# mLSTM prompt/sample kernel: the sample states' matmuls stand between the K steps of the next projections, and attention's last stores are asked for ahead of the late weight loads

## The chip, the core and the metric

One core of one Trainium2 chip runs the whole kernel in one launch. The metric is device time in microseconds (us) from one execution of it. TensorE (PE) does matmuls, VectorE (DVE) and ScalarE (ACT) evict and scale, GpSimd (POOL) does elementwise work and issues a few transfers, SyncE (SP) issues nearly all others.

## What is computed

A decoder layer for a prompt of 2048 tokens (with 16 meta tokens ahead) and, with the same weights, 8 sample sequences of 8 tokens each:

```
p = RMSNorm_pre(x) @ w_in + b_in        # q_a k_a v_a z_a | q_m k_m v_m o_m z_m i_m f_m | g_a g_b
y_a = sliding_window_attention(...) * silu(z_a)               # 16 heads, 4 kv heads
# mLSTM, 4 heads of width 256, per chunk; C0 is the matrix memory (256 x 256), n0 its normaliser
num = a * (q @ C0) + (W * q k^T) @ v
den = a * (q @ n0) + rowsum(W * q k^T)
h   = num / max(|den|, exp(-m))
C1  = aL * C0 + (k * wL)^T @ v ;  n1 = aL * n0 + sum(k * wL)
y_m = sigmoid(o_m) * h * silu(z_m)
out = x + RMSNorm_post((sigmoid(g_a) * (y_a @ w_pa) + sigmoid(g_b) * (y_m @ w_pb)) @ w_out)
```

Every sample sequence has its own C0 and n0 for each mLSTM head (32 states of 256 x 256), which are read, used, updated and stored. The prompt starts at zero and carries one state per head through its 17 tiles.

## The kernel before

The rows are 17 tiles of 128. Tile 0 is the mixed one: 16 meta tokens in rows 0 to 15, the 64 sample rows in rows 64 to 127 (`S0 = 64`); tiles 1 to 16 are the prompt. There are four stages, one after the other: `prelude` (norm, gates), `mlstm` (4 heads x 17 tiles), `attention` (4 kv heads x 17 tiles) and `tail` (merge and output products). Every engine has its own program, in order, and only semaphores tie them together; nothing is scheduled for them.

In `mlstm` each engine walks through slots (h, t), with n = 17 h + t. In slot n, PE first projects tile n+1 in three blocks (`block_a`: q and k into bank `p_a`; `block_b`: v and o into `p_b`; `block_c`: z into `p_c`), and between the blocks it does tile n: transposes of q and k (L1118), the product q k^T (L1126), then the reads of the state and the sum over the tile into `p_n` (L1142, L1143) and the update of the state into `p_u` (L1147). A block is 8 K steps; a K step is three matmuls (L642 to L644: high by high, high by low, low by high part), 512 columns wide in blocks a and b and 256 in block c. A [128 x 128] by 257-column fp32 matmul is two records in the profile.

Slot t = 0 is different (`mixed_tile`). After block_c come the tile's own sum (L1152), the meta tokens' update of the prompt state (L1157), and then, for each of the 8 sequences b, two matmuls that read its state into `p_n` (L1166: the weights `qz` hold q of that sequence alone in 64 columns, the output is rows 64 to 127) and two that make its update (L1179: 64 rows of `kwz` by `vaug`) into `p_u`, or into `p_a` and `p_b` for even b. DVE applies each update to `cs` (L1017) and moves the normaliser column in and out (`ncol`, L1058; L1025). Only then does PE go on to slot 1, whose `block_a` comes first. I call the two reads or the two updates of one sequence a pair: 16 pairs a head, 64 in all.

DVE in slot t = 0: `evict_a`, `qat` (L976), `wlog` (L978), eight copies into `qz` (L985), `evict_b`, ..., the copies of the meta update into `cn` (L1008, semaphore `c_ready`), the 8 sequences' updates, then the denominator and `y` (L1028 to L1038).

POOL in slot n makes the low part of tile n+2's h (`pool_split_h`, L635; slot n+1's `block_a` waits for it). In slot t = 0 of heads 0 to 2 it waits until the 8 states are stored (`cs_out`) and issues the loads of the next head's 8 (`load_states`, L889). Then it prepares weights for `tail`, two or three chunks a slot (`prepare`, L910 to L925). SP stores a sample state when its update is ready, in slot t = 0 (L802), loads h, stores y, and so on, in one queue.

At the end of `attention`, SP's slot t = 16 of the last head asks for the rest of the tail's first weights (8 transfers, 6 MB, `k.late_in`), then stores the last keys and values, then the last `y`; it waits for the landing of those stores (L1383, L1384) before the barrier ahead of `tail` (L2639). PE waits for `late_in` at its fifth product.

Of the kernel before, what the change touches and what calls it, by code (L numbers as in the profile page):

```python
# [54 lines left out]
W_COLS = 5 * MD  # L55
STG = 4
# [582 lines left out]
def project(nc, out, hi, lo, k, col, n):  # L639

    for j in range(KT):
        nc.tensor.matmul(out, hi[:, j], k.w_hi[:, j, col:col + n], start=(j == 0), stop=False)  # L642
        nc.tensor.matmul(out, hi[:, j], k.w_lo[:, j, col:col + n], start=False, stop=False)  # L643
        last = nc.tensor.matmul(out, lo[:, j], k.w_hi[:, j, col:col + n], start=False, stop=(j == KT - 1))  # L644
    return last


def mlstm(nc, k):
# [3 lines left out]
    with ExitStack() as ctx:  # L652
# [28 lines left out]
        qz = sb("ml_qz", [P, NB, JD, NB * DT])  # L681
# [20 lines left out]
        qz_ready, kwz_ready, us_done, cs_ready = sem("qz_ready"), sem("kwz_ready"), sem("us_done"), sem("cs_ready")  # L702
        qz_clear = sem("qz_clear")
# [8 lines left out]
        last_n = MH * NT - 1  # L712
        block = ctx.enter_context(nc.Block())
# [16 lines left out]

        def sample_banks(b):

            return p_u if b % 2 else [p_a, p_b]
# [8 lines left out]
        def _(sp):  # L742
# [24 lines left out]
            def slot(h, t, n, u, half):  # L767
# [30 lines left out]
                if isinstance(t, int) and t == 0:  # L798
# [85 lines left out]
        def _(pool):  # L884
            nc.gpsimd.memset(qz[:, :, :, :], 0.0).then_inc(qz_clear, 1)
# [46 lines left out]
        def _(dve):  # L932
# [28 lines left out]
            def slot(h, t, n, u, half):  # L961
# [40 lines left out]
                if tile0:  # L1002
# [7 lines left out]
                    for b in range(NB):  # L1010
                        c = NB * h + b
                        if b == 0:
                            for bb in range(2):
                                ncol(NB * h + bb)
                        dve.wait_ge(us_done, c + 1)
                        for j in range(JD):
                            q = V.scalar_tensor_tensor(out=cs[:, b, j, :], in0=cs[:, b, j, :],  # L1017
                                                       scalar=k.al_smp[:, b, h:h + 1],
                                                       in1=sample_banks(b)[j][:, 0:MD + 1],
                                                       op0=ALU.mult, op1=ALU.add)  # L1020
                        q.then_inc(cs_ready, 1)
                        if b + 2 < NB:
                            ncol(c + 2)
                        dve.wait_ge(cs_ready, c + 1)
                        V.tensor_copy(nout[:, :, b * MH + h], cs[:, b, :, MD]).then_inc(nout_ready, 1)  # L1025
# [14 lines left out]
                if not tile0:  # L1040
# [12 lines left out]
            def ncol(c):  # L1053

                b, h = c % NB, c // NB
                if h:
                    dve.wait_ge(nout_ready, (NB + 1) * (h - 1) + b + 1)
                V.tensor_copy(cs[:, b, :, MD], k.n0_col[:, :, b * MH + h]).then_inc(ncol_ready, 1)  # L1058
# [11 lines left out]
        def _(pe):  # L1070
# [6 lines left out]
            def proj_ab(h, n, u, bank, col, width, done, free, nchunks):  # L1077
# [6 lines left out]
                project(nc, bank[:, 0:width], k.h_hi[:, u], k.h_lo[:, u], k, col, width).then_inc(done, 1)  # L1084

            def block_a(h, n, u, new):
                proj_ab(h, n, u, p_a, A, 2 * MD, proj_a, qk_ready, 4 if new else None)

            def block_b(h, n, u, new):
# [16 lines left out]
            def slot(h, t, n, u, half):  # L1106
# [4 lines left out]
                if more:  # L1111
                    block_a(hn, n + 1, 1 - u, last)
# [1630 lines left out]
```

## Time and profile before

| | |
|---|---|
| median of 3 runs | 3233.28 us (3232.41, 3233.28, 3253.26) |
| the profiled execution | 3260.61 us, span 3258.7 us |
| PE busy | 3099.0 us, 95% of the span |
| DVE, POOL, ACT busy | 1485.8, 1264.9, 1040.1 us |
| mean granted TensorE clock | 0.953 of full |

The profile is of one execution, which took 27.3 us longer than the median of the runs. The span is from the first to the last instruction; the other 1.9 us lie around it. A busy share is no measure of need: at half clock PE is busy twice as long for the same work.

### The profile page before, as it was taken

To read this page: it belongs to the slowest core of one execution; us is meant where nothing else is said; L and a number is where in the kernel's file an instruction comes from. 1 tells how busy PE (TensorE), PEld (TensorE's weight loads), DVE (VectorE), ACT (ScalarE), POOL (GpSimd) and SP (SyncE) were. 2 spreads that over 40 slices of the span, in tenths; PEclk is the share of its full clock that TensorE was granted. 3 is DMA by queue.
4 is the path that set the end of the run, shared out by engine and by line. 5 is a ranking of instruction groups with operands and counts; after the bars stand their busy time and mean duration, and the time that the engine had idled before them with its cause. 6 is when DMAs were issued, how large, how long until landed. Compare 5 with 4: busy or idle time off the path is not lost. (4 is left out here: it accounts for less than half of the span.)

```text
span 3258.7 us, 51503 instructions
## 1 busy us (share of the span) xinstructions
PE 3099.0 (95%) x17011; PEld 2648.1 (81%) x17011; DVE 1485.8 (46%) x3684; ACT 1040.1 (32%) x2450; POOL 1264.9 (39%) x938
## 2 busy tenths in 40 slices
PE   5799999999899999989999999999979999999898
PEld 4578877888688878878989989989868787878787
DVE  3323342335333523345455555545445464546487
ACT  5211121113111311124444444434423333333343
POOL 2235544554445535211212212212244444546566
PEclk8789997999999979999999999989989999999999
DMA  8644454435634534241121121141152847377843
GB/s 251 186 141 145 145 166 159 141 133 149 206 127 144 161 120 146 77 124 54 54 74 62 56 79 56 48 145 56 54 212 108 331 161 293 122 273 248 298 155 136
DMA packets 259046, 472.27 MB, mean 145 GB/s; under 512 B 29778, under 2 KB 138855, under 8 KB 255812
## 3 DMA queue, kind: packets, MB, share of 16 engines
q1 hardware_dynamic: 254692, 461.08, 42.0%
q0 software_dynamic: 2880, 8.93, 0.9%
q8 instruction: 70, 1.15, 0.1%
q10 hardware_dynamic: 1344, 0.62, 0.1%
q14 instruction: 60, 0.49, 0.1%
HBM read 316.15 MB, written 156.38 MB: 145 GB/s over the span
## 5 line engine op out<-in xcount | busy, mean ns | idle before, releaser
L635 POOL TENSOR_TENSOR a_all<-h_raw,a_all 128x1024 fp32r<-128x1024 f32 x137 | 329.1, 2402 | 803.9 <-issue 453.9
L839 ACT ACTIVATE ml_qkt<-ml_pt 128x512 f32<-128x512 f32 x68 | 40.8, 600 | 974.3 <-PE ml_pt L1118 974.3
L2418 DVE TENSOR_TENSOR a_all<-tl_sums,a_all 128x512 fp32r<-128x512 f32 x165 | 186.4, 1130 | 219.7 <-ACT a_all L2314 218.5
L642 PE MATMUL ml_pa<-w_all,a_all 128*128 128x512 f32 x544 | 230.8, 424 | 25.9 <-issue 17.1
L943 DVE TENSOR_TENSOR ml_qk<-ml_pa,ml_bias 128x512 f32<-128x512 f32 x68 | 47.1, 692 | 425.7 <-ACT ml_kw L843 420.7
L642 PE MATMUL ml_pb<-w_all,a_all 128*128 128x512 f32 x544 | 217.5, 400 | 3.4 <-issue 3.4
L644 PE MATMUL ml_pa<-w_all,a_all 128*128 128x512 f32 x544 | 217.5, 400 | 0.0
L643 PE MATMUL ml_pa<-w_all,a_all 128*128 128x512 f32 x544 | 217.4, 400 | 0.0
L644 PE MATMUL ml_pb<-w_all,a_all 128*128 128x512 f32 x544 | 212.1, 390 | 0.0
L643 PE MATMUL ml_pb<-w_all,a_all 128*128 128x512 f32 x544 | 212.0, 390 | 0.0
L1401 POOL TENSOR_TENSOR at_vs<-at_qkv,ones 128x64 f32<-128x64 f32 x68 | 22.0, 323 | 475.9 <-PE at_bank_po L1765 466.0
L1443 ACT ACTIVATE at_sm<-at_sm,at_nmx 128x272 f32<-128x272 f32 x272 | 138.8, 511 | 180.3 <-DVE at_nmx L1592 180.3
L925 POOL TENSOR_TENSOR w_early<-prep_raw,w_early 128x512 fp32r<-128x512 f32 x140 | 188.5, 1346 | 11.2
L642 PE MATMUL at_bank_pa<-w_all,a_all 128*128 128x384 f32 x544 | 189.2, 348 | 0.0
L627 ACT ACTIVATE a_all<-h_raw 128x1024 fp32r<-128x1024 f32 x137 | 144.0, 1052 | 127.8 <-DMA h_raw<-h_t 127.8
L643 PE MATMUL at_bank_pa<-w_all,a_all 128*128 128x384 f32 x544 | 181.9, 334 | 0.0
L644 PE MATMUL at_bank_pa<-w_all,a_all 128*128 128x384 f32 x544 | 181.9, 334 | 0.0
L2574 PE MATMUL tl_bank_y<-w_all,a_all 128*128 128x512 f32 x416 | 167.0, 401 | 13.0 <-DMA w_all<-w_split 13.0
L642 PE MATMUL at_bank_pb<-w_all,a_all 128*128 128x256 f32 x544 | 165.0, 303 | 3.0 <-PEq L652 3.0
L2577 PE MATMUL tl_bank_y<-w_all,a_all 128*128 128x512 f32 x416 | 164.8, 396 | 0.0
L2576 PE MATMUL tl_bank_y<-w_all,a_all 128*128 128x512 f32 x416 | 164.8, 396 | 0.0
L642 PE MATMUL ml_pc<-w_all,a_all 128*128 128x256 f32 x544 | 159.1, 292 | 0.0
(406 smaller groups left out, 8657.9 us busy)
## 6 DMA issues: line engine op xcount, KB each, us to landing
h_raw<-h_t SPq DMA_DIRECT2D x140, 512.0 KB, 4.3
w_split<-w_early SPq DMA_DIRECT2D x140, 512.0 KB, 3.0
w_all<-w_split SPq DMA_DIRECT2D x36, 1024.0 KB, 11.2
stage<-w_in_in SPq DMA_DIRECT2D x35, 512.0 KB, 7.2
w_early<-w_split SPq DMA_DIRECT2D x14, 1024.0 KB, 10.1
stage_more<-w_in_in SPq DMA_DIRECT2D x21, 512.0 KB, 7.3
w_all<-w_split SPq DMA_DIRECT2D x20, 512.0 KB, 10.5
tl_w<-w_split SPq DMA_DIRECT2D x10, 1024.0 KB, 8.3
```

The lines of the kernel that those rows point to most:

```text
L627: nc.scalar.activation(k.h_hi[:, u], k.h_raw[:, u], ACT.Copy).then_inc(k.h_hi_ready, 1)
L635: nc.gpsimd.tensor_tensor(k.h_lo[:, u], k.h_raw[:, u], k.h_hi[:, u].bitcast(F32), ALU.subtract).then_inc(k.h_lo_ready, 1)
L642: nc.tensor.matmul(out, hi[:, j], k.w_hi[:, j, col:col + n], start=(j == 0), stop=False)
L643: nc.tensor.matmul(out, hi[:, j], k.w_lo[:, j, col:col + n], start=False, stop=False)
L644: last = nc.tensor.matmul(out, lo[:, j], k.w_hi[:, j, col:col + n], start=False, stop=(j == KT - 1))
L925: G.tensor_tensor(prep_split[:, c % 2, 1], prep_raw[:, j], prep_split[:, c % 2, 0].bitcast(F32), ALU.subtract).then_inc(prep_lo, 1)
L943: V.tensor_tensor(qk[:, :], p_a[:, :], bias[:, h % 2, A:B], ALU.add).then_inc(qk_ready, 1)
L1443: nc.scalar.activation(sm[:, g, :], sm[:, g, :], ACT.Exp, bias=nmx[:, g:g + 1], scale=HD ** -0.5, accum_out=rs[:, g:g + 1]).then_inc(exp_r ...
L2418: V.tensor_tensor(a_part(q, 1), operand(g, j), hi, ALU.subtract).then_inc(a_lo, 1)
L2574: T.matmul(bank_of(bank, at), hi, w_row(at, 0, t), start=fresh and t == 0, stop=False, skip_group_check=True)
L2576: T.matmul(bank_of(bank, at), hi, w_row(at, 1, t), start=False, stop=False, skip_group_check=True)
L2577: last = T.matmul(bank_of(bank, at), lo, w_row(at, 0, t), start=False, stop=t == KH - 1, skip_group_check=True)
```

## The change

In mLSTM the two matmuls that read the state of sequence b move in slot 0 from behind block_c to a place between K steps: b = 0 to 4 ahead of K steps 3 to 7 of `block_b`, b = 5 to 7 ahead of K steps 0 to 2 of `block_c`. The first one now starts the accumulation in `p_n` over all 128 rows (its weights have zeros in the other columns), and the tile's own sum ends it. The two matmuls of the update of sequence b move to slot 1, ahead of K step b of its `block_a`, and all go into `p_u`, each half with a semaphore of its own. PE's program of mLSTM is written out instead of looped.

With that: DVE fills `qz` in one copy and the normaliser column in one (ahead of `evict_b`), applies the updates after `y`, and copies the new normalisers out in one; SP stores the sample states in slot 1; POOL loads the next head's states in slot 4. In attention SP asks for the last `y` store first and for the eight late loads after it, and the waits for the landing of the stores move into `tail`.

```diff
-            nc.gpsimd.memset(qz[:, :, :, :], 0.0).then_inc(qz_clear, 1)
+            nc.gpsimd.memset(qz[:, :], 0.0).then_inc(qz_clear, 1)
...
                 pool_split_h(nc, k, n + 2, u, (proj_c, n + 1))
-                if isinstance(t, int) and t == 0 and h + 1 < MH:
+                if isinstance(t, int) and t == 4 and h + 1 < MH:
+                    pool.wait_ge(nout_ready, 2 * h + 1)
                     pool.wait_ge(cs_out, 16 * NB * (h + 1))
                     load_states(h + 1)
...
-                    for b in range(NB):
-                        q = V.tensor_copy(qz[:, b, :, DT * b:DT * (b + 1)], qat[:, :, S0 + DT * b:S0 + DT * (b + 1)])
-                    q.then_inc(qz_ready, 1)
+                    V.tensor_copy(own_rows, qat[:, :, S0:P].rearrange("p j (b t) -> p b j t", t=DT)).then_inc(qz_ready, 1)
+                    if h:
+                        dve.wait_ge(nout_ready, 2 * (h - 1) + 1)
+                    V.tensor_copy(cs[:, :, :, MD], n0_head(h)).then_inc(ncol_ready, 1)
...
-                if not tile0:
+                if tile0:
+                    for b in range(NB):
+                        c = NB * h + b
+                        for j in range(JD):
+                            dve.wait_ge(us_done if j else us_half, c + 1)
+                            V.scalar_tensor_tensor(out=cs[:, b, j, :], in0=cs[:, b, j, :],
+                                                   scalar=k.al_smp[:, b, h:h + 1], in1=p_u[j][:, 0:MD + 1],
+                                                   op0=ALU.mult, op1=ALU.add).then_inc(cs_ready if j else cs_half, 1)
...
-                    block_a(hn, n + 1, 1 - u, last)
+                    block_a(hn, n + 1, 1 - u, last, (lambda j: state_updates(h, j)) if t == 1 else None)
+                if t == 1:
+                    pe.sem_inc(u_done, 1)
...
-                    block_b(hn, n + 1, 1 - u, last)
+                    block_b(hn, n + 1, 1 - u, last, (lambda j: sample_rows(h, n, j - 3)) if tile0 else None)
...
+            def sample_rows(h, n, b):
+                if not 0 <= b < NB:
+                    return
+                if b == 0:
+                    pe.wait_ge(qz_ready, h + 1)
+                    pe.wait_ge(ncol_ready, h + 1)
+                    pe.wait_ge(cs_in, 16 * NB * (h + 1))
...
+            def state_updates(h, b):
+                c, n = NB * h + b, NT * h
+                pe.wait_ge(n_done, n + 1)
+                pe.wait_ge(kwz_ready, c + 1)
+                for j in range(JD):
                     if b == 0:
                         pe.wait_ge(c_ready, n + 1)
                     else:
-                        pe.wait_ge(cs_ready, c - 1)
...
+                        pe.wait_ge(cs_ready if j else cs_half, c)
+                    T.matmul(p_u[j][:, 0:MD + 1], kwz[S0:P, b, j * P:(j + 1) * P], k.vaug[S0:P, n % 2, :],
+                             start=True, stop=True).then_inc(us_done if j else us_half, 1)
-            run_steps(pe, MH, slot)
+            all_steps(MH, slot)
...
             sp.dma_start(y_dram(KVH - 1, NPT), yt[:, last_m % 2]).then_inc(y_out[last_m % 2], 16)
-            for s in y_out:
-                sp.wait_ge(s, 16 * (last_m + 1) // 2)
-            sp.wait_ge(kv_out, 16 * KVH * (2 * NB + 4))
+            sp.wait_ge(proj_a, last_m + 1)
+            sp.wait_ge(proj_b, last_m + 1)
+            for slot in range(4, N_PAIR):
+                for part in range(2):
+                    load_block(sp, k, 0, slot, part, None, k.late_in)
```

PE, end of slot 0 and start of slot 1 of head 0, before (`ml_pn` is the bank p_n, `ml_pu`, `ml_pa` and `ml_pb` are p_u, p_a and p_b):

```order
192 L644 MATMUL ml_pc<-w_all,a_all 128x256
193 L1152 MATMUL ml_pn<-vaug,ml_wqk 128x257
194 L1157 MATMUL ml_pu<-vaug,ml_kw 128x257 x2
195 L1166 MATMUL ml_pn<-ml_cs,ml_qz 64x257 x2
196 L1179 MATMUL ml_pa<-vaug,ml_kwz 128x257
197 L1179 MATMUL ml_pb<-vaug,ml_kwz 128x257
198 L1166 MATMUL ml_pn<-ml_cs,ml_qz 64x257 x2
199 L1179 MATMUL ml_pu<-vaug,ml_kwz 128x257 x2
```

The same place in the changed kernel:

```order
201 L647 MATMUL ml_pc<-w_all,a_all 128x256
202 L1173 MATMUL ml_pn<-vaug,ml_wqk 128x257
203 L1179 MATMUL ml_pu<-vaug,ml_kw 128x257 x2
204 L1193 MATMUL ml_pu<-vaug,ml_kwz 128x257 x2
205 L645 MATMUL ml_pa<-w_all,a_all 128x512
206 L646 MATMUL ml_pa<-w_all,a_all 128x512
207 L647 MATMUL ml_pa<-w_all,a_all 128x512
208 L1193 MATMUL ml_pu<-vaug,ml_kwz 128x257 x2
```

No read stands there any more, and each pair of updates is followed by a K step of the next tile's block_a. The first pair still stands right behind the meta update.

PE in block_b of slot 0, in the changed kernel (before, these are K steps alone):

```order
150 L645 MATMUL ml_pb<-w_all,a_all 128x512
151 L646 MATMUL ml_pb<-w_all,a_all 128x512
152 L647 MATMUL ml_pb<-w_all,a_all 128x512
153 L1168 MATMUL ml_pn<-ml_cs,ml_qz 128x257
154 L1168 MATMUL ml_pn<-ml_cs,ml_qz 64x257
155 L645 MATMUL ml_pb<-w_all,a_all 128x512
156 L646 MATMUL ml_pb<-w_all,a_all 128x512
157 L647 MATMUL ml_pb<-w_all,a_all 128x512
158 L1168 MATMUL ml_pn<-ml_cs,ml_qz 64x257 x2
```

The first read, 128 rows of output wide, stands ahead of K step 3 and waits for DVE's copies and the loaded states; all that follows in block_b is queued behind it.

POOL in head 0, slot 0 before, where the loads of head 1's states stand ahead of the next tile's low part (`a_all`):

```order
25 L635 TENSOR_TENSOR a_all<-h_raw,a_all 128x1024
26 L889 DMA ml_cs<-state_C_in 128x2x256 x8
27 L635 TENSOR_TENSOR a_all<-h_raw,a_all 128x1024
28 L923 CAST w_early<-prep_raw 128x512
29 L925 TENSOR_TENSOR w_early<-prep_raw,w_early 128x512
```

POOL in the changed kernel, slots 4 and 5 of head 0:

```order
46 L636 TENSOR_TENSOR a_all<-h_raw,a_all 128x1024
47 L897 DMA ml_cs<-state_C_in 128x2x256 x8
48 L932 CAST w_early<-prep_raw 128x512
49 L934 TENSOR_TENSOR w_early<-prep_raw,w_early 128x512
50 L919 TENSOR_TENSOR prep_raw<-prep_raw 128x512
51 L932 CAST w_early<-prep_raw 128x512
52 L934 TENSOR_TENSOR w_early<-prep_raw,w_early 128x512
53 L636 TENSOR_TENSOR a_all<-h_raw,a_all 128x1024
```

The loads and a slot's weight preparation now stand together between two low parts.

## Rows read from the trace of the kernel before

**Rows 1.** Who waited for whom, PE: total us, times, longest
```profile
PE ml_pa L642 <- issue: 17.1, 3, 10.6
```
**Rows 2.** Windows, one a head: slot 0's L1152 to slot 2's L1099
```profile
147.07:211.55 64.48, 59.77 (x189) 38.60 (x187) 17.42 (x54) 4.20 (x8) 15.47 (x15) 0.68 0.37 119
479.42:544.07 64.65, 59.94 (x189) 38.35 (x188) 17.20 (x54) 4.20 (x8) 22.32 (x22) 0.68 0.55 175
811.96:868.05 56.09, 42.96 (x188) 30.53 (x187) 17.64 (x54) 4.20 (x8) 22.34 (x22) 0.91 0.74 232
1135.94:1195.03 59.09, 56.62 (x188) 36.55 (x187) 16.88 (x54) 4.04 (x8) 17.88 (x15) 0.71 0.40 137
```
**Rows 3.** Timeline, PE, ordinary tiles of head 0: start us, us, what
```profile
408.63 1.03 PE L1142 MATMUL ml_pn<-ml_cn,ml_qat 128*128 128x257 f32 x4
409.50 0.59 PE L1143 MATMUL ml_pn<-vaug,ml_wqk 128*128 128x257 f32 x2
...
416.27 0.38 PE L1099 MATMUL ml_pc<-ident,ml_y 128*128 128x128 f32 x2
...
433.33 0.38 PE L1099 MATMUL ml_pc<-ident,ml_y 128*128 128x128 f32 x2
```
**Rows 4.** Timeline, PE, sample loop of head 2, at full clock
```profile
814.70 1.05 PE L1166 MATMUL ml_pn<-ml_cs,ml_qz 128*64 128x257 f32 x4 [1.08 <-DVE ml_cs L1058]
...
828.04 1.05 PE L1166 MATMUL ml_pn<-ml_cs,ml_qz 128*64 128x257 f32 x4 [0.86 <-DVE ml_cs L1058]
...
832.82 0.49 PE L642 MATMUL ml_pa<-w_all,a_all 128*128 128x512 f32 x1 [0.59 <-PE ml_pu L1179]
```
**Rows 5.** Timeline, PE, sample loop of head 0 and block_a behind it
```profile
160.28 1.97 PE L1166 MATMUL ml_pn<-ml_cs,ml_qz 128*64 128x257 f32 x4
...
181.64 0.63 PE L642 MATMUL ml_pa<-w_all,a_all 128*128 128x512 f32 x1
182.92 0.63 PE L642 MATMUL ml_pa<-w_all,a_all 128*128 128x512 f32 x1
```
**Rows 6.** Timeline, slot 0 of head 2: K step 3, DVE's qz copies
```profile
805.25 0.39 PE L642 MATMUL ml_pb<-w_all,a_all 128*128 128x512 f32 x1
...
805.72 0.71 DVE L985 COPY ml_qz<-ml_qat 128x16 f32<-128x16 f32 x8
```
**Rows 7.** Tile ml_cs to 150 us; head 0: last load, K step 3
```profile
DMA to landing us min/median/max: 5.3/6.7/8.1
...
136.42 1.44 POOL L889 DMA_DIRECT2D ml_cs<-state_C_in  x2 [7.70 <-issue]
...
140.36 0.39 PE L642 MATMUL ml_pb<-w_all,a_all 128*128 128x512 f32 x1
```
**Rows 8.** Timeline: state loads (last of head 0's; head 2); ordinary slot
```profile
200.03 0.74 POOL L889 DMA_DIRECT2D ml_cs<-state_C_in  x1 [5.46 <-issue]
...
840.62 2.16 POOL L889 DMA_DIRECT2D ml_cs<-state_C_in  x3 [12.75 <-DMA o_s_c<-ml_cs]
...
851.49 1.44 POOL L889 DMA_DIRECT2D ml_cs<-state_C_in  x2 [3.29 <-issue]
...
623.71 0.58 PE L642 MATMUL ml_pa<-w_all,a_all 128*128 128x512 f32 x1
...
634.16 2.38 POOL L635 TENSOR_TENSOR a_all<-h_raw,a_all 128x1024 fp32r<-128x1024 f32 x1 [9.16 <-issue]
```
**Rows 9.** Windows, POOL alone: a low part and three chunks
```profile
634.10:645.60 11.50, 10.85 (x9) 1.00 0.46 146
```
**Rows 10.** Timeline and one line of code, end of attention
```profile
2359.71 2.42 SPq L1954 DMA_DIRECT2D w_all<-w_split  x4
2362.17 9.44 SPq L1951 DMA_DIRECT2D w_all<-w_split  x4
...
2365.51 0.38 ACT L1493 ACTIVATE at_yt<-at_bank_pb 128x256 f32<-128x256 f32 x1 [5.00 <-PE at_bank_pb L1707]
...
L1383 SPq EVENT_SEMAPHORE  x1: 4999/4999/4999, 2375.1 to 2375.1; - x1
```

More of the change, by code:

```diff
@@ L55 @@
 W_COLS = 5 * MD
+QZ_DIAG = JD * NB * DT + 2 * DT
 STG = 4
@@ L636, in pool_split_h, with project @@
                             ALU.subtract).then_inc(k.h_lo_ready, 1)
-def project(nc, out, hi, lo, k, col, n):
+def project(nc, out, hi, lo, k, col, n, between=None):
     for j in range(KT):
+        if between is not None:
+            between(j)
         nc.tensor.matmul(out, hi[:, j], k.w_hi[:, j, col:col + n], start=(j == 0), stop=False)
@@ L797, in slot @@
                         load_chunk(sp, k, k.ML[h] + 10 + c)
-                if isinstance(t, int) and t == 0:
+                if isinstance(t, int) and t == 1:
                     for b in range(NB):
@@ L1009, in slot @@
                     q.then_inc(c_ready, 1)
[L1010 to L1025, printed above, removed]
                 dve.wait_ge(n_done, n + 1)
@@ L1075, in weights, with proj_ab @@
                 pe.wait_ge(k.w_lo_ready, k.ML[h] + done)
-            def proj_ab(h, n, u, bank, col, width, done, free, nchunks):
+            def proj_ab(h, n, u, bank, col, width, done, free, nchunks, between=None):
                 if nchunks is not None:
@@ L1083, in proj_ab, with block_a, block_b, block_c @@
                     pe.wait_ge(free, n)
[L1084 to L1089, printed above, removed]
-                proj_ab(h, n, u, p_b, B, 2 * MD, proj_b, vo_ready, 8 if new else None)
-            def block_c(h, n, u, new):
-                proj_ab(h, n, u, p_c, C, MD, proj_c, z_ready, 10 if new else None)
+                project(nc, bank[:, 0:width], k.h_hi[:, u], k.h_lo[:, u], k, col, width,
+                        between).then_inc(done, 1)
+            def block_a(h, n, u, new, between=None):
+                proj_ab(h, n, u, p_a, A, 2 * MD, proj_a, qk_ready, 4 if new else None, between)
+            def block_b(h, n, u, new, between=None):
+                proj_ab(h, n, u, p_b, B, 2 * MD, proj_b, vo_ready, 8 if new else None, between)
+            def block_c(h, n, u, new, between=None):
+                proj_ab(h, n, u, p_c, C, MD, proj_c, z_ready, 10 if new else None, between)
             def y_transposed(n):
@@ L1130, in slot @@
                         pe.wait_ge(yt_ready, n)
-                    block_c(hn, n + 1, 1 - u, last)
+                    block_c(hn, n + 1, 1 - u, last, (lambda j: sample_rows(h, n, 5 + j) if j < 3 else None) if tile0 else None)
                 pe.wait_ge(wqk_ready, n + 1)
@@ L1356, in slot @@
                             load_block(sp, k, 0, slot, part, None, early_in)
-                if is_last(t) and a + 1 == KVH:
-                    sp.wait_ge(proj_a, m + 1)
-                    sp.wait_ge(proj_b, m + 1)
-                    for slot in range(4, N_PAIR):
-                        for part in range(2):
-                            load_block(sp, k, 0, slot, part, None, k.late_in)
                 if isinstance(t, int) and t == 0:
@@ L2086, in load_raw @@
                 s, t, n = g // N_ITEM, tile_rows(g)[0], len(tile_rows(g))
+                if g == N_ITEM * PA:
+                    for y_out in k.at_y_out:
+                        sp.wait_ge(y_out, 16 * KVH * NT // 2)
                 if s == OUT:
@@ L2210, in _ @@
             sp.wait_ge(single_out, 16 * 3)
+            sp.wait_ge(k.at_kv_out, 16 * KVH * (2 * NB + 4))
         @block.gpsimd
```

60 lines of the change are left out of this document (26 added, 34 removed).

## Prediction, made before the changed kernel was run

> **What bounds the kernel now.** I read the shares of the engines on the page first: PE is busy for 3099.0 of 3258.7 us, DVE for 46%, POOL for 39%, ACT for 32%. So PE bounds it, and there is no other engine whose saved time would shorten anything by itself. A busy PE is still not a fast PE, so the next view was the granted clock by slice, which is below full in slices of mLSTM; then PE's own waits, where one line stands out among projections, 17.1 us in 3 waits [rows 1]; then one window for each head from L1152 in slot 0 to L1099 in slot 2, which takes in everything that the change moves in mLSTM. The four windows last 64.48, 64.65, 56.09 and 59.09 us at a granted clock of 0.68, 0.68, 0.91 and 0.71 [rows 2]: three heads run the sample work near half clock (1.2 GHz of 2.4), head 2 near full.
>
> What would that stretch last without sample work? An ordinary tile repeats every 17.06 us (L1099 at 416.27 and 433.33), and from the tile's own read to the L1099 behind it is 7.64 us, of which the read pair takes 0.87 [rows 3]. So 7.64 − 0.87 + 17.06 = 23.8 us. The four windows sum to 244.3; 4 × 23.8 = 95.3 would be needed. **149.0 us** lie above it. They are the 64 read pairs and 64 update pairs, DVE waits ahead of them, half clock in them and in the block_a behind them, and the three gaps of [rows 1], which stand ahead of slot 2's block_a: there POOL's low part comes late, since POOL issues eight state loads ahead of it. The sum takes all 149.0 away and puts back what the changed kernel needs.
>
> **Part 1, the pairs: +76.8.** At full clock a pair of 257-column matmuls with 128 rows and columns takes 0.87 [rows 3]. In head 2's sample loop 16 pairs run from 814.70 to 832.82 = 18.12 us, less waits of 0.86 and 0.59 = 16.67, or 1.04 a pair [rows 4]. Each pair there is followed by one of another tile shape (64 output columns, then 64 contraction rows), so I read 0.17 as the price of one change of shape. In the changed kernel every pair stands between K steps of full shape: two changes, 0.87 + 2 × 0.165 = 1.20, and 64 pairs (8 reads and 8 updates in each of 4 heads) make 76.8. The lower end is one change's price for both, about 0.95 to 1.04: 61 to 67. The upper end is that the next weights can't be loaded under such a matmul: half as much again as the loop's 1.04, 1.6 a pair, 102. I take 1.20, since it is nearest to the row with the same operands. One 128-row read a head changes nothing.
>
> The Trainium skill ("TensorEngine Tiling (Array Packing)", Key Properties) says that changing the tiling mode needs TensorE drained first, without a price. By it the 0.17 is the drain and the alternation costs it 128 times, as above; if the drain of a 512-column matmul is longer than that of a 257-column one, the sum would be the upper end. No row before the change shows it between these projections.
>
> **Part 2, new waits inside the projections: +7.2 and +2.2.** The first read of a head stands ahead of K step 3 of block_b and waits for DVE. In head 2 that K step starts at 805.25, and DVE begins the qz copies at 805.72 [rows 6]; now one copy does (a few tenths: I take 0.2) and one for the normaliser column (0.16), so it is ready near 806.1. That is 0.85 of PE idle a head, 3.4 in all; all later K steps queue behind it. DVE's evict_b starts some tenths later, which block_a of the next slot hides. The first update of a head waits for DVE's copies of the meta update (`c_ready`). Head 2 waited 1.08 behind that update, for those copies and a normaliser column [rows 4]; without the column, 0.13, that is 0.95 a head, 3.8. Later updates wait for DVE's update of the half before, which has a K step (0.68 at full clock) and the other half to be done in, so nothing. Before them DVE has y to make, about 1.1 us behind `c_ready`, against 0.87 + 0.68 on PE: covered, by 0.4. 3.4 + 3.8 = 7.2.
>
> Head 0 has one more: its states. POOL issues the last two loads at 136.42 for 1.44 us and a load lands 5.3 to 8.1 us after its issue [rows 7], so at 142.4 to 144.2 at the earliest; PE gets to K step 3 of block_b at 140.36 [rows 7], where before it needed these states only at 160.28 [rows 5]. That is a stall of 2.1 to 3.8; about 2.0 beyond the 0.85, and 0.2 for a qz memset one fifth longer, which stands ahead of the loads: **+2.2**.
>
> **Part 3, POOL's loads in slot 4: +5.5.** The three gaps go, as slot 0 and 1 now have a low part and preparation only. But in slot 4 POOL issues the loads: 840.62 to 851.49 + 1.44 = 12.3 us in head 2 [rows 8], and up to 17.4 in head 0, where the last of them alone had 5.46 of issue ahead of it [rows 8]. It then prepares two or three chunks; a low part and three chunks fill 11.50 us [rows 9], 2.4 of it the low part [rows 8], so 9.1 for three and 6 for two. In an ordinary slot the low part starts 634.16 − 623.71 = 10.5 us behind the slot's first matmul and takes 2.38 [rows 8]: it ends at 12.8. The next low part is needed two slots on, at 2 × 17.06 = 34.1. Head 1 has three chunks in slot 4: 12.8 + 12.3 + 9.1 + 2.4 = 36.6, 2.5 late. Head 0 and 2 have two: 12.8 + 15 to 17 + 6 + 2.4 = 36 to 38 in head 0, 2 to 4 late; 33.5 in head 2, in time. With a half-clock tail behind one of them I put **+5.5**; the ends are 0 (POOL idles enough in the slots before to be early) and 17.1, the old gaps again. The wait for `cs_out` is met: SP stores the states in slot 1 and they land in slot 2. SP's 32 stores there cost it 0.4 each, and its load of h is not due until slot 3.
>
> **Part 4, end of attention: −1.8.** Now SP issues the late loads from 2359.71 for 2.42 + 9.44 = 11.9 us, then the last y store, and waits 5.0 us for its landing, from 2375.1 to 2380.1 [rows 10], and the tail begins behind that. In the changed kernel yt is ready at 2365.9 [rows 10], the store goes first, then 11.9 + 0.6 of issue: SP is free at 2378.4 instead of 2380.1. The late loads start 6 us later and land near 2387; PE wants them at its fifth product, near 2393. Bounds: −6, if what bounds the barrier is ready when the store would be, and +3, if loads of bias and raw rows come late behind them.
>
> **Part 5, PE's loops written out: 0.** Tail's PE is written out already and its slots are full; ordinary tiles in the loop repeat at the same 17.06 as those outside it.
>
> **The sum.** 3260.6 − 149.0 + 76.8 + 7.2 + 2.2 + 5.5 − 1.8 = **3201.5**, with every head at full clock. Will they be? At half clock a pair lasts 1.97 [rows 5] and a K step 1.28 (181.64 to 182.92 [rows 5]), against 0.68. Three heads of four had fallen by the time of their loop, one, with a wait of the same size [rows 4], had not. That wait stays, at the same place; what stood behind it was a stretch of pairs alone, and now stands K steps' 512 columns. I take one head to fall there: 8 × (1.97 − 1.20) + 8 × (1.28 − 0.68) = 6.2 + 4.8 = 11, and 2 until it rises, **+13**. Forecast: **3214.5**.
>
> The profiled execution lies 27.3 us above the median. If heads 0 and 1 had run as head 2 did, each window would be 8.5 shorter, and head 3 about 15 shorter (it has no gap behind it): that makes 3228 for an all-full-clock execution, and the three runs of 3232 to 3253 lie between it and 3260.6. So I take the 27 us to be clock in stretches whose old price the sum has removed whole, and don't shift the forecast by it.
>
> **Rivals.** (1) Full clock throughout, and the 27 us lie elsewhere in the kernel: 3201.5 less up to 27: 3175 to 3200. Head 2 speaks for it: sample work alone doesn't lower the clock. Against it: heads 0, 1 and 3. (2) Changes of shape are dear: 1.6 a pair, 102 − 77 = +25: 3240. The loop's 0.17 speaks against it, but it is a change between two small shapes. (3) The other side, slower: the wait for qz in block_b (0.85 us, more in head 0) lowers the clock there, and it stays low through reads, block_c, meta update, its wait and the updates up to the y transposes. Then each of four heads pays 8 × 0.77 + 8 × 0.6 = 11 for reads and their K steps and 13 for the updates, near 24: 4 × 24 = 97, 3201.5 + 97 = 3298. It is slower than 3266 if more than 64 us are lost so, that is if three heads run both parts at half clock. Against it: an idle PE of 0.86 in head 2's loop left the clock high [rows 4]. (4) The change doesn't do what it says for the gaps: all 17.1 come back in slot 6: 3201.5 + 11.6 + 13 = 3226.
>
> **Chances.** Forecast (3201 to 3228) 0.55; rival 1 0.22; rival 2 0.10; rival 3 0.08; rival 4 0.05. A measurement of this kernel can tell about 1%, 32 us: faster is below 3201, slower above 3266. Faster: rival 1, and a quarter of the forecast's case, where no head falls: 0.36. Slower: rival 3, 0.08. Same: 0.56. The range 3188 to 3243 holds the forecast's case, rival 2 and 4, and half of rival 1.
>
> **What would show it.** In the profile after: reads in block_b 1.88 apart (1.20 + 0.68) at full clock and 3.3 at half; PE idle of 0.8 ahead of the first read, 2 to 4 in head 0; the gaps ahead of slot 2's block_a gone, and small ones ahead of slot 6's; four windows of L1152 to slot 2's L1099 near 23.8 + 9.6 + 1 = 34 us each (40 for one that falls); PE's idle time between attention and tail 1.8 us shorter. The prediction is wrong if a pair between K steps costs over 1.4 at full clock, if two or more heads fall (13 each), if the weight loads of a K step behind a small matmul are exposed, or if POOL is more than 5 us late in slot 6.

## The result and the profile after

The changed kernel takes 3254.55 us (median of 20 runs, 3233.08 to 3267.51), the kernel before 3236.31 (20 runs, 3213.89 to 3264.79): a ratio of 1.005 with a 95% interval of 1.0026 to 1.0074. It is slower by a little, where 3214.5, a gain of 22 us, was forecast. The profiled execution took 3259.87 us with a span of 3258.0; the profile before was of 3260.61.

Most terms of the sum can be read in the profile after. First the PE timeline of head 0 and head 1 around the reads and the first updates:

```profile
144.14 1.25 PE L1168 MATMUL ml_pn<-ml_cs,ml_qz 128*128 128x257 f32 x4 [2.41 <-DMA ml_cs<-state_C_in]
145.32 0.77 PE L645 MATMUL ml_pb<-w_all,a_all 128*128 128x512 f32 x1
...
146.87 1.97 PE L1168 MATMUL ml_pn<-ml_cs,ml_qz 128*64 128x257 f32 x4
148.78 0.50 PE L645 MATMUL ml_pb<-w_all,a_all 128*128 128x512 f32 x1
...
474.90 1.25 PE L1168 MATMUL ml_pn<-ml_cs,ml_qz 128*128 128x257 f32 x4 [0.72 <-DVE ml_qz L993]
...
476.99 1.08 PE L1168 MATMUL ml_pn<-ml_cs,ml_qz 128*64 128x257 f32 x4
...
478.91 1.08 PE L1168 MATMUL ml_pn<-ml_cs,ml_qz 128*64 128x257 f32 x4
...
494.99 1.10 PE L1193 MATMUL ml_pu<-vaug,ml_kwz 64*128 64x257 f32 x4 [1.87 <-POOL a_all L636]
496.02 0.50 PE L645 MATMUL ml_pa<-w_all,a_all 128*128 128x512 f32 x1
...
496.92 2.08 PE L1193 MATMUL ml_pu<-vaug,ml_kwz 64*128 64x257 f32 x4
498.92 0.79 PE L645 MATMUL ml_pa<-w_all,a_all 128*128 128x512 f32 x1
...
500.50 2.08 PE L1193 MATMUL ml_pu<-vaug,ml_kwz 64*128 64x257 f32 x4
```

A read pair and its K step repeat every 478.91 − 476.99 = 1.92 us, so a pair costs 1.92 − 0.68 = 1.24 at full clock: the 1.20 of the sum, against 1.04 in the old loop [rows 4]. In head 0 the 2.41 us wait for the states is followed by a few us at half clock (K step and pair at 145.3 to 148.8), and then the clock rises again although narrow reads (64 output columns) still stand there. The updates go another way. One pair after the wait of 1.87 the period is 500.50 − 496.92 = 3.58 us and stays so to the end of block_a. The windows view of that stretch (duration, PE busy, instructions, granted clock, DMA share, GB/s):

```profile
496.92:521.89 24.97, 24.97 (x51) 0.50 0.11 43
```

PE is busy without a pause and has half its clock. That happens in all four heads of this execution. The waits view, PE:

```profile
PE tl_bank_x L2583 <- PEq L2649: 14.4, 1, 14.4
...
PE ml_pu L1193 <- POOL a_all L636: 6.0, 2, 4.1
...
PE ml_pn L1168 <- DMA ml_cs<-state_C_in: 2.4, 1, 2.4
...
PE ml_pn L1168 <- DVE ml_qz L993: 2.2, 3, 0.7
...
PE ml_pu L1193 <- DVE ml_cn L1018: 2.0, 2, 1.0
```

The first line is the wait between attention and tail. The three gaps ahead of slot 2 are gone ([rows 1] has them). In their place is a wait ahead of the first update pair: 0.94 and 1.01 in heads 0 and 3, for `c_ready` as before, but 1.87 and 4.08 in heads 1 and 2 for POOL's low part of tile 2, which the prediction didn't foresee. Its cause stands on the SP and ACT timelines of head 1, slot 0:

```profile
467.55 3.42 SPq L746 DMA_DIRECT2D ml_bias<-b_in_in  x5
471.07 5.47 SPq L210 DMA_DIRECT2D stage_more<-w_in_in  x4
476.63 7.92 SPq L210 DMA_DIRECT2D stage<-w_in_in  x4
484.64 1.69 SPq L620 DMA_DIRECT2D h_raw<-h_t  x1
...
491.36 1.06 ACT L628 ACTIVATE a_all<-h_raw 128x1024 fp32r<-128x1024 f32 x1 [13.72 <-DMA h_raw<-h_t]
```

SP asks for 13 pieces of the next head's biases and weights first, for 16.8 us, and only then for h. It lands at 491.3, ACT and POOL need 1.06 and 2.34 us more, and block_a waits. In head 2 POOL is held longer still: it waits 23.2 us for the landing of a store of prepared weights, which SP asks for behind the same 13 requests and h. Before, the same queue stood there, and the sample loop, 17 to 31 us long, hid it.

The windows view once more, from block_b of slot 0 (head 0) or slot 0's y transposes (heads 1 to 3) to slot 2's y transposes, which takes in reads, updates and all waits of both kernels. After:

```profile
139.42:211.44 72.02, 68.67 (x241) 45.03 (x240) 20.58 (x49) 9.30 (x21) 9.90 (x7) 0.76 0.38 116
471.31:540.09 68.78, 66.19 (x245) 44.03 (x244) 19.27 (x49) 9.57 (x22) 19.41 (x18) 0.80 0.59 174
800.29:873.72 73.43, 68.64 (x246) 45.45 (x245) 19.91 (x49) 9.57 (x22) 16.81 (x14) 0.77 0.61 184
1132.19:1201.60 69.41, 67.68 (x246) 44.81 (x245) 21.10 (x49) 9.57 (x22) 18.17 (x15) 0.78 0.51 158
```

Before, the same stretches:

```profile
138.20:211.55 73.35, 68.64 (x242) 46.51 (x240) 20.95 (x70) 9.32 (x21) 15.47 (x15) 0.72 0.47 141
469.99:544.07 74.08, 69.37 (x246) 46.83 (x245) 20.73 (x70) 9.58 (x22) 24.45 (x25) 0.72 0.61 185
802.54:868.05 65.51, 52.38 (x245) 39.00 (x244) 21.17 (x70) 9.58 (x22) 22.34 (x22) 0.92 0.78 235
1126.52:1195.03 68.51, 66.04 (x245) 45.02 (x244) 20.41 (x70) 9.58 (x22) 17.88 (x15) 0.75 0.51 159
```

Head 2, which had kept its clock before, loses 7.9 us and head 3 0.9; heads 0 and 1 gain 1.3 and 5.3. The sums of the four are 281.4 before and 283.6 after.

### The profile page after: what moved, and what is told of

Its sections match the earlier page's. It is cut to its first block and busy times, and to the rows that moved or that the text cites. A ratio compares the mean times of both kernels' runs of the same rounds, so it can differ in the third digit from the quotient of the medians.

```text
span 3258.0 us, 51239 instructions
## 1 busy us (share of the span) xinstructions
PE 3107.8 (95%) x17011; PEld 2644.5 (81%) x17011; DVE 1494.3 (46%) x3600; ACT 1038.4 (32%) x2450; POOL 1263.7 (39%) x938
## 5 line engine op out<-in xcount | busy, mean ns | idle before, releaser
L645 PE MATMUL ml_pa<-w_all,a_all 128*128 128x512 f32 x544 | 237.2, 436 | 9.3 <-PEq L252 3.9
L645 PE MATMUL ml_pb<-w_all,a_all 128*128 128x512 f32 x544 | 222.2, 408 | 3.4 <-issue 3.4
L647 PE MATMUL ml_pa<-w_all,a_all 128*128 128x512 f32 x544 | 220.3, 405 | 0.0
L646 PE MATMUL ml_pa<-w_all,a_all 128*128 128x512 f32 x544 | 219.5, 404 | 0.0
L646 PE MATMUL ml_pb<-w_all,a_all 128*128 128x512 f32 x544 | 214.0, 393 | 0.0
L647 PE MATMUL ml_pb<-w_all,a_all 128*128 128x512 f32 x544 | 213.8, 393 | 0.0
L628 ACT ACTIVATE a_all<-h_raw 128x1024 fp32r<-128x1024 f32 x137 | 144.0, 1052 | 127.1 <-DMA h_raw<-h_t 127.1
## 6 DMA issues: line engine op xcount, KB each, us to landing
w_early<-w_split SPq DMA_DIRECT2D x14, 1024.0 KB, 10.2
```

What stands on the lines that cost most here:

```text
L628: nc.scalar.activation(k.h_hi[:, u], k.h_raw[:, u], ACT.Copy).then_inc(k.h_hi_ready, 1)
```

## The experiments

Four theories are named in what follows. T1: idle time ahead of the updates lowers the clock. T2: the update pairs themselves, which use 64 of the array's 128 rows, lower it. T3, which came out of the first four edits: an idle time starts the fall and 64-row pairs behind it hold the clock down; either alone doesn't. T4: narrow reads next to an idle time do the same.

Where a kernel is called so many us less than the changed kernel, that is against its median of 3254.55, which was taken on another occasion. The kernel before had 3236.31 beside that one, and 3243.84 (29 runs; with h_first, full_rows, upd_b and reads_back) and 3242.24 (22 runs; with before_full, att_back_full, shift_h and best1) beside the later ones. So such a difference is uncertain by some 7 us, and the ratios to the kernel before, each taken on one occasion, are the firmer numbers.

Three executions of unedited kernels stand first, since the median and the profile before differed by 24 us. They were run last, and their expectations already speak of T3.

> The kernel before, unedited, for another profile. T3 says that its time follows the number of heads whose sample loop falls to half clock: three of four in the profile of 3260.6. In an execution near the median of 3236 one or two should have fallen, 8 to 15 us each, and nothing else should differ between the two executions.

> The same again. Rival: the heads fall in every execution and the 24 us between median and profile lie outside mLSTM's slots 0 to 2; then three heads are at half clock here too, whatever the time.

> The changed kernel, unedited, for another profile. T3 and the spread of its runs (3233 to 3268): three or four heads fall to half clock at their updates, about 14 us each; an execution near 3254 has all four or three.

They took 3265.80, 3247.47 and 3250.99 us; none of the three profiles of before lies at the median of 3236. The table has the time from slot 0's to slot 2's y transposes, read from the timelines; a star marks a head whose sample work ran at half clock (granted 0.50, read in windows of 5 us; shorter dips are not starred), a fallen head in what follows. Head 0 has no slot ahead of its own to start from: its times run from block_b of slot 0 and are given for the first profiles alone.

| execution | us | head 0 | head 1 | head 2 | head 3 |
|---|---|---|---|---|---|
| before | 3260.6 | 73.4* | 74.1* | 65.5 | 68.5* |
| before, second profile | 3265.8 | full | 74.1* | 75.1* | 69.0* |
| before, third profile | 3247.5 | full | 62.3 | 76.0* | 70.0* |
| after | 3259.9 | 72.0* | 68.8* | 73.4* | 69.4* |
| after, second profile | 3251.0 | full | 68.4* | 73.9* | 69.5* |

The theory has the time follow the number of fallen heads: two at 3247, three at 3261 and 3266. The rival (three in each, and the difference elsewhere) doesn't hold. In the kernel before, head 1 takes 62 us at full clock and 74 when fallen, head 2 65.5 and 75 to 76, and head 3 (full clock by the full-row run below) 53 and 69 to 70. A fallen head after (68.4 to 73.9) is slower than a full-clock head before (62.3, 65.5). Whether the change pays is a matter of how many heads fall.

Head 0 of the second profile of after is the changed kernel's work at full clock, behind the same wait of 0.94 us:

```profile
167.25 1.13 PE L1193 MATMUL ml_pu<-vaug,ml_kwz 64*128 64x257 f32 x4
...
169.21 1.13 PE L1193 MATMUL ml_pu<-vaug,ml_kwz 64*128 64x257 f32 x4
```

The period is 1.95 to 1.96 us, so a 64-row update pair costs 1.27. From its first update to slot 2's y transposes that head takes 32.6 us, and the fallen head 0 of the first profile 46.6: a fall costs 14.0 us.

**Full-row updates.** `kwz` is zero outside a sequence's eight rows, so the matmul may as well take all 128 rows:

```
-  T.matmul(p_u[j][:, 0:MD + 1], kwz[S0:P, b, j * P:(j + 1) * P], k.vaug[S0:P, n % 2, :],
+  T.matmul(p_u[j][:, 0:MD + 1], kwz[:, b, j * P:(j + 1) * P], k.vaug[:, n % 2, :],
```

> The update matmuls take all 128 rows of kwz and vaug instead of 64 (the rows outside a sequence are zeros in kwz, the result is the same). No change of tile shape is left around them. Both theories: an update pair costs 0.87 instead of 1.20 at full clock and about 1.75 instead of 2.1 at half clock. T1 (the idle time ahead of them lowers the clock): all four heads fall as in the changed kernel; 32 pairs save 0.35 each, about 11 us: 3243. T2 (64-row matmuls pull the clock down): no head falls, 4 x 14 us more come back: 3190.

It took 3201.28 us (3199.3 to 3209.85), 53 less than the changed kernel and 0.987 (0.985 to 0.990) of the kernel before. T1 had said 3243 and T2 3190. PE, head 1, behind the same kind of wait:

```profile
484.78 1.10 PE L1193 MATMUL ml_pu<-vaug,ml_kwz 128*128 128x257 f32 x4 [1.95 <-POOL a_all L636]
485.54 0.58 PE L645 MATMUL ml_pa<-w_all,a_all 128*128 128x512 f32 x1
...
486.68 1.92 PE L1193 MATMUL ml_pu<-vaug,ml_kwz 128*128 128x257 f32 x4
488.03 0.99 PE L645 MATMUL ml_pa<-w_all,a_all 128*128 128x512 f32 x1
...
489.61 1.03 PE L1193 MATMUL ml_pu<-vaug,ml_kwz 128*128 128x257 f32 x4
...
491.17 1.03 PE L1193 MATMUL ml_pu<-vaug,ml_kwz 128*128 128x257 f32 x4
```

The clock still falls behind the wait, within the first K step, but now it is back 3 us later, where 64-row pairs kept it down for 25 us and more. Head 2, behind a wait of 4.30, dips for 7 us; heads 0 and 3 (0.94 and 1.01) don't dip. At full clock the period is 1.57 instead of 1.95: a pair costs 0.89, so the two changes of shape cost 0.38 a pair. That is 12 of the 53 us; the rest is clock. No head fell in this profile; this refutes T1 as written, by which the wait alone held the clock down.

The edit takes away two things at once: the half-used rows and the changes of shape around the updates. Which of them holds the clock down is settled further down, by full rows in the kernel before.

**Updates in block_b of slot 1.**

```
-  block_a(hn, n + 1, 1 - u, last, (lambda j: state_updates(h, j)) if t == 1 else None)
+  block_a(hn, n + 1, 1 - u, last)
...
-  block_b(hn, n + 1, 1 - u, last, (lambda j: sample_rows(h, n, j - 3)) if tile0 else None)
+  block_b(hn, n + 1, 1 - u, last,
+          (lambda j: sample_rows(h, n, j - 3)) if tile0 else (lambda j: state_updates(h, j)) if t == 1 else None)
```

(DVE's update loop moves to slot 1, behind `wlog`, and DVE's program is written out.)

> The updates move from block_a of slot 1 to block_b of slot 1, still one pair ahead of each K step, and VectorE applies them in slot 1 behind wlog; block_a of slot 1 then covers the wait for c_ready. T1 (idle time ahead of the updates lowers the clock): heads 0 and 3 have no idle time any more and stay at full clock (13 to 14 us each), heads 1 and 2 still wait about 3 to 5 us for the low part ahead of block_a and may fall there, over block_a's own 512-column K steps (5 us) and the updates: 3254 less 28 to 56, 3200 to 3226. T2 (the update pairs themselves): the clock falls a few us behind the first update in block_b in all heads, and only the 4 x 0.95 come back: 3250.

3238.56 us (3234.55 to 3254.91), 16 less than the changed kernel and 0.999 (0.997 to 1.001) of the kernel before; neither T1's 3200 to 3226 nor T2's 3250. Heads 0 and 3 kept full clock, as T1 had it, though their update pairs have 64 rows: that refutes T2 alone. Heads 1 and 2 fell. PE in head 1:

```profile
480.28 0.47 PE L645 MATMUL ml_pa<-w_all,a_all 128*128 128x512 f32 x1 [1.47 <-issue]
481.04 0.53 PE L645 MATMUL ml_pa<-w_all,a_all 128*128 128x512 f32 x1
482.23 0.63 PE L645 MATMUL ml_pa<-w_all,a_all 128*128 128x512 f32 x1
483.50 0.63 PE L645 MATMUL ml_pa<-w_all,a_all 128*128 128x512 f32 x1
484.69 0.40 PE L645 MATMUL ml_pa<-w_all,a_all 128*128 128x512 f32 x1
...
491.39 2.05 PE L1194 MATMUL ml_pu<-vaug,ml_kwz 64*128 64x257 f32 x4 [1.17 <-DVE ml_cs L1002]
...
494.95 2.08 PE L1194 MATMUL ml_pu<-vaug,ml_kwz 64*128 64x257 f32 x4
```

The wait ahead of block_a gives a dip of three K steps that ends by itself; the clock is full from 484.7. The new wait of 1.17 between the first and second pair is followed by half clock to the end of the updates. The expectation had put the fall down to the first wait, which was wrong. Heads 0 and 3 had the same new wait (1.03 and 1.17) and didn't fall, and head 2 fell behind 1.17: a wait of about 1 us ahead of such pairs doesn't always do it, and its length doesn't decide it.

So the theory became T3. Two kernels took it from either side.

**Waits shortened, rows left at 64.** SP asks for the next head's biases and chunks last in slot 0, and each update stands one K step later:

```
-  block_a(hn, n + 1, 1 - u, last, (lambda j: state_updates(h, j)) if t == 1 else None)
+  block_a(hn, n + 1, 1 - u, last, (lambda j: state_updates(h, j - 1) if j else None) if t == 1 else None)
   if t == 1:
+      state_updates(h, NB - 1)
```

> The changed kernel with 64-row updates, with two waits shortened: in slot 0 SyncE asks for the next head's biases and weight chunks last, behind the load of h, the prepared weights' stores and y; and the update of sequence b stands ahead of K step b+1, the last one behind K step 7, so that block_a's first K step (0.7 us) covers c_ready. Idle time ahead of the updates is then about 0.3 us behind a K step and 0 to 0.5 ahead of it, in all four heads. T3 (idle time and 64-row pairs together): few or no heads fall, 3254 less 45 to 60: 3195 to 3210. T2 (64-row pairs alone): all fall, only the idle time comes back, 8 us: 3246.

3200.94 us (3197.38 to 3215.05), 0.989 (0.985 to 0.992) of the kernel before. PE in head 0:

```profile
160.53 1.13 PE L1180 MATMUL ml_pu<-vaug,ml_kw 16*128 16x257 f32 x4
161.59 0.50 PE L645 MATMUL ml_pa<-w_all,a_all 128*128 128x512 f32 x1
...
162.60 1.10 PE L1194 MATMUL ml_pu<-vaug,ml_kwz 64*128 64x257 f32 x4
163.63 0.50 PE L645 MATMUL ml_pa<-w_all,a_all 128*128 128x512 f32 x1
...
164.52 1.13 PE L1194 MATMUL ml_pu<-vaug,ml_kwz 64*128 64x257 f32 x4
```

It lies within T3's 3195 to 3210; T2 would have had 3246. No wait is left ahead of the updates, and the profile shows full clock through all four heads, also behind the waits for `qz` (0.72, and 1.72 in head 2). Heads 1 to 3 take 54.6, 55.6 and 54.6 us. The pairs are those of the changed kernel (period 1.92 to 1.96). One thing more came with the new order: head 0's states land by 139.8 instead of 144.0, before the first chunk load is asked for (146.3; 126.8 in the changed kernel), and the wait for them (2.41) is gone.

**Full rows in the kernel before** (L1179, the same edit):

> The kernel before with one edit: its update matmuls take all 128 rows of kwz and vaug. After the first runs the theory is T3: the clock falls where an idle time of about 1 us or more stands ahead of 64-row update pairs; either alone leaves it up. Here the 1 to 1.9 us wait ahead of the sample loop stays, and the narrow reads (64 output columns) too. T3: the heads don't fall any more, 10 to 20 us off: 3225. T4 (narrow reads next to an idle time do it as well; the changed kernel only looks safe there because K steps stand between): heads fall as before, 3243 less the shape changes, at most 5 us: 3240.

3217.68 us (3214.79 to 3227.45), 0.995 (0.992 to 0.998) of the kernel before, and below T3's 3225. No sample loop stayed at half clock; heads 1 to 3 take 62.0, 66.4 and 53.1. The wait of 1.0 to 2.2 us ahead of the loop stood there still, and so did the reads of 64 columns, so T4 (3240) falls. Head 2 dipped behind its wait and came back:

```profile
790.32 1.89 PE L1166 MATMUL ml_pn<-ml_cs,ml_qz 128*64 128x257 f32 x4 [1.09 <-DVE ml_cs L1058]
792.14 1.23 PE L1179 MATMUL ml_pa<-vaug,ml_kwz 128*128 128x257 f32 x2
...
794.00 1.08 PE L1166 MATMUL ml_pn<-ml_cs,ml_qz 128*64 128x257 f32 x4
```

This also parts rows from shape. The loop has as many changes of shape as in the kernel before (every read pair is followed by an update pair of another shape, still 1.04 a pair), and only the rows of the updates differ. With 64 rows 8 of 12 loops in the three profiles of before ran at half clock to their end; with 128 rows none of four did, and the 12 runs lie within 13 us of each other. So it is the half-used rows that hold the clock down and not the changes of shape. Why they do is not shown.

It is also a fairer price of the whole change, with no fallen head in either kernel: 3217.7 against 3201.3, 16 us. In that difference are the three gaps ahead of slot 2, which before_full still has (6.5, 5.9 and 10.2 us), so it is not the price of the interleaving alone.

**The load of h first in slot 0**, with all else as in the changed kernel:

```
   if isinstance(t, int) and t == 0:
+      next_h(t, n, u)
       if h + 1 < MH:
```

(`next_h` holds the call of `load_h`, which is left out further down where t is 0.)

> SyncE's load of the tile after next is issued first in slot 0, ahead of the bias and weight chunk loads of the next head; all else is the changed kernel. In the changed kernel the first update pair of heads 1 and 2 waited 1.87 and 4.08 us for POOL's low part of that tile, against 0.94 and 1.01 in heads 0 and 3, where c_ready was last. Both theories expect those two waits at 0.95 if this queue is the cause (about 4 us off); head 2's may keep a part if the store of prepared weights is what holds POOL. Theory T1 (the idle time of 0.9 to 4 us ahead of the updates lowers the clock): a gap of 0.95 stays, so all four heads still fall to half clock there. T2 (the 64-row update pairs themselves pull the clock down): all four fall too. Time: the changed kernel's less 3 to 5 us, 3250.

3248.27 us (3232.52 to 3264.16), 6 less than the changed kernel and 1.002 (0.999 to 1.004) of the kernel before, which these runs can't tell from the changed kernel's 1.005. The profile tells more: head 1's wait for the low part is gone (0.94 for `c_ready` is left), head 2's is still 4.5. There POOL waits 23.6 us until SP's store of prepared weights has landed, also behind the chunk loads. Only when all of SP's work in slot 0 went ahead of the chunks (shift_h) did both go. Heads 0 to 2 fell behind 0.94, 0.94 and 4.5 us of idle time, head 3 with 1.01 did not.

**The reads together again**, behind block_c:

```
-  block_b(hn, n + 1, 1 - u, last, (lambda j: sample_rows(h, n, j - 3)) if tile0 else None)
+  block_b(hn, n + 1, 1 - u, last)
...
   def mixed_tile(h, n, u):
+      for b in range(NB):
+          sample_rows(h, n, b)
```

> The eight read pairs of a head stand together behind block_c again, ahead of the tile's own sum; the updates stay between K steps. T1 and T2 both: the reads cost 0.87 to 1.04 a pair if the clock is full there (16 x 2 changes of shape less: 32 pairs x 0.2 to 0.3 = 6 to 10 us off), the 0.72 us wait for qz ahead of the reads goes (3 x 0.7 + 2.4 in head 0 = 4.5), so up to 14 us faster than the changed kernel: 3241. If a row of narrow reads next to the wait lowers the clock earlier, the reads run at 1.97 a pair and that gain is lost: 3255 to 3265.

3241.85 us (3237.94 to 3256.77), 13 less than the changed kernel, 1.001 (0.999 to 1.003) of the kernel before, and at the expected 3241. PE in head 1:

```profile
474.64 7.26 PE L1168 MATMUL ml_pn<-ml_cs,ml_qz 128*128 128x257 f32 x32
481.82 0.70 PE L1175 MATMUL ml_pn<-vaug,ml_wqk 128*128 128x257 f32 x2
...
488.89 2.05 PE L1195 MATMUL ml_pu<-vaug,ml_kwz 64*128 64x257 f32 x4 [5.30 <-POOL a_all L636]
```

Eight pairs take 7.2 us, 0.90 each against 1.24 between K steps, and no wait for `qz` is left: 32 × 0.34 + 4.6 = 15 us less by these rows. Part of it comes back as idle time: heads 1 and 2 now wait 5.30 and 7.58 us for POOL's low part instead of 1.87 and 4.08, since less work stands ahead of it. All four heads fell, so the reads had no part in that. At 1.24 a pair between K steps, against 0.90 together and 1.04 in the old loop, putting reads between K steps was a loss by itself; moving both together from the loop had hidden that.

**The end of attention as before**, on the full-row kernel (late loads back ahead of the last stores, the waits back ahead of the barrier):

> The changed kernel with full-row updates (3201.3 before this), with its attention end as in the kernel before: late weight loads first, then the last stores, and their landing awaited there. Full rows are used since the runs then lie within 10 us. The prediction says that the new order is worth 1.8 us: 3203; the idle time of PE between attention and tail 16.5 instead of 14.7. Rival: late loads that start 6 us later cost it back at tail's fifth product: 3201 or below.

3200.99 us (3199.15 to 3204.45), against 3201.28 with the change: no difference that these runs can tell, so they decide neither for the expected 3203 nor for the rival. In the profile PE's idle time ahead of the tail is 16.1 us there and 14.7 with the change, 1.4 us apart, so the order of requests gives about the 1.8 that was said; in the time of the kernel it is lost in the noise.

**Both cures together**, full rows and shortened waits:

> The same two edits and full-row updates. All theories: 3201.3 less the idle time that goes (4.3 + 2.0 + 2 x 1.0 less about 4 x 0.3): 3193 to 3195. Rival: the chunk loads of the next head, asked for later, come late for VectorE's and ScalarE's splits in slots 15 and 16, or SyncE's queue holds slot 1's load of h: back to 3200.

3187.08 us (3182.66 to 3190.42), 0.985 (0.980 to 0.990) of the kernel before: the fastest here, 67 below the changed kernel. It is 6 to 8 us better than the expected 3193 to 3195, and the rival (3200) doesn't hold. In the profile, heads 1 to 3 take 51.7, 52.7 and 51.8 us, where full_rows has 55.1, 58.6 and 52.5; that is 10 us, and part of it are the dips behind the waits, which the expectation had left out. It had left out head 0's states too: with the chunk loads behind them the last one lands at 138.9 instead of 148.0, and PE waits 0.71 for `qz` instead of 4.21 for the states.

## Why the prediction was wrong

**The sum at full clock was nearly right.** 3201.5 was worked out for a kernel in which no head falls. No run of the changed kernel shows that, but three numbers bear on it. The kernel with the same 64-row pairs and no fallen head (shift_h) took 3200.9, with 8 us less waiting than the changed kernel: near 3209. The two profiles of the changed kernel, less 14.0 for each fallen head, give 3259.9 − 56 = 3204 and 3251.0 − 42 = 3209. The sum with the 4 us of the overlooked wait (below) is 3205.5. Term by term: a pair 1.20, measured 1.22 to 1.24 for reads and 1.27 for updates, 3 us more in all; the wait for `qz` 0.85 a head, 0.72; head 0's states 2.2 beyond that, 2.41 in all, so 1.7; `c_ready` 0.95, 0.94 and 1.01 where it was last; the wait ahead of slot 6 5.5 in all, 3.2 in the first profile (18.49 and 18.80 against the period of 17.06 in heads 0 and 1, nothing in head 2) and 5.55 in the second; the end of attention 1.8, 2.1 by the waits view (16.5 before, 14.4 after). That the misses of opposite sign nearly cancel is luck.

**The step that failed is "I take one head to fall there".** Four fell in the profiled execution, three in the second. At half clock a pair and its K step take 3.58 instead of 1.95, so eight cost 13.0 us and the whole fall 14.0, near the 13 of the text: 3205.5 + 4 × 14 = 3261.5, and 3259.9 was measured. The 40 us between the forecast and the median of 3254.55 are two to three more fallen heads and the overlooked wait. The text argued that K steps of full shape behind the wait would spare most heads. Against [rows 4] and [rows 5] that was a guess: they show only that a loop after such a wait can go either way. The runs show that 64-row updates hold a lowered clock down even with a K step between any two of them, and that one edit to 128 rows frees it. Why one head falls and another with the same wait doesn't stays open.

**Slips in its numbers.** The sign for a fallen head, a window of 40 us, doesn't follow from the text's own price: 34 + 13 = 47. Measured are 35.2 for the one at full clock and 48.3 to 53.8 for the fallen ones. And the half-clock price adds 1.97 of the old loop to a K step of 1.28, 3.25 in all; between K steps it was 3.58, so such a pair costs 2.30. In Part 2 the last load, issued at 137.1, would land by 145.2 at the latest and not by 144.2; in runs with the same order of requests PE waited 2.0 to 4.7 for the states.

**A wait was overlooked.** h of tile 2 comes late in SP's queue, behind 13 requests. The text cleared SP's stores in slot 1 and POOL's queue in slot 4, but didn't ask what the removed loop had hidden in slot 0. It cost 1.87 and 4.08 where 0.95 was counted, 4 us. Heads 1 and 2 (the long waits) and head 3 (1.01) fell in both profiles of the changed kernel, head 0 (0.94) in one of two.

**The comparison with the median.** The text put the 27 us between profile and median down to heads that didn't fall, and estimated 3228 for an execution with none. The three profiles of before bear out the first (two fallen heads at 3247.5, three at 3260.6 and 3265.8), and its full-row version, at 3217.7 with the same price of a pair, says that none fallen is lower than 3228. So at its median the kernel before has, by these prices, one or two fallen heads, and the changed one three or four: +18 us, while the two first profiles show the same time.

**The rivals.** Rival 3 came nearest: half clock on the other side. It had the place half right (updates yes, reads no) and so was priced at 97 instead of 56. The sentence against it, that 0.86 us of idle time left the clock high in head 2, was true of that wait, and of 0.73 and 0.97 inside loops of the second and third profile; but in both of these head 2 fell behind the 1.08 ahead of its loop. Rival 1 needed full clock throughout, and rival 4 all the gaps in slot 6; neither came. Rival 2's 1.6 a pair is refuted by 1.24 and 1.27: the two changes of shape around a pair cost 0.34 us (reads of 64 columns) and 0.38 us (updates of 64 rows). By the Trainium skill ("TensorEngine Tiling (Array Packing)", Key Properties) a change of tiling mode drains TensorE; it gives no price, and the trace agrees in that every change costs something.

## What to carry to other kernels

Before a long low-priority stretch is taken out of a critical path, list what else finished under its cover (here a queue of 13 requests ahead of one that the next step needs). A matmul that uses half of the array's rows was no cheaper than a full one here (1.27 us a pair against 0.89 between K steps), and it kept a clock down that an idle time of 1 us or more had lowered; with operands padded by zeros, one edit was worth 53 us of 3254. And where executions differ in how many stages fell, compare kernels by the count of fallen stages and the price of each, not by one profile of each.

## What the runs showed of the hardware

- Behind 20 waits ahead of 64-row update pairs (five profiles: both of after, upd_b, h_first, reads_back) 16 ended in half clock, which began during the wait or within 2 us of its end: all seven of 1.55 to 7.58 us, and nine of thirteen of 0.94 to 1.17 us. With those pairs between K steps the clock stayed at half through 25 us of unbroken work.
- The short waits went both ways at the same length: 0.94 (fell: head 0 of after and of h_first; not: head 0 in the second profile of after), 1.01 (fell: head 3 of after; not: head 3 of h_first), 1.17 (fell: heads 1 and 2 of upd_b; not: head 3 of upd_b). What decides there stays open.
- Behind waits with work of full rows, the clock dipped in some cases and was back after 3 to 7 us (full_rows, heads 1 and 2; upd_b, block_a of heads 1 and 2; before_full, head 2, with 64-column reads in the loop; head 0 of after and of full_rows, with 64-column reads between K steps). In others it didn't dip at all (1.74 us, head 1 of att_back_full; 2.64 us, head 0 in the second profile of after).
- 64-row update pairs with no wait ahead didn't lower it (shift_h, four heads).
- A 257-column pair costs 0.88 to 0.90 next to its own kind or as a full-shape pair between K steps, and 1.22 to 1.27 between K steps of another shape.
